# Triangular inverses by 64x64 tiles, eight units a step, with a separate last doubling

## What is computed

```python
# gated delta rule, per head and chunk
a = jnp.where(strict, jnp.einsum("bhncd,bhnsd->bhncs", k_beta, k) * decay, 0.0)
t_inv = lax.linalg.triangular_solve(eye + a, jnp.broadcast_to(eye, a.shape), left_side=True, lower=True)
u = jnp.einsum("bhncs,bhnse->bhnce", t_inv, v_beta)
w = jnp.einsum("bhncs,bhnsd->bhncd", t_inv, k_beta * jnp.exp(g)[..., None])
...
# RWKV-7, per head and token; in chunks it needs such an inverse too
sa = jnp.einsum('bhvk,bhk->bhv', state, a_t)
state = state * w_t[:, :, None, :] + sa[..., None] * b_t[:, :, None, :] + v_t[..., None] * k_t[:, :, None, :]
```

## Time and profile before

| | |
|---|---|
| median of 3 runs | 1961.89 us (1960.22 to 1963.19) |
| the profiled execution | 1957.99 us |
| its span (first to last instruction) | 1956.3 us |
| PE busy | 1835.5 us, 94% |
| PE weight load busy | 1558.4 us, 80% |
| DVE busy | 1059.6 us, 54% |
| ACT busy | 893.8 us, 46% |
| POOL busy | 170.7 us, 9% |
| four batches of the delta rule | about 812 to 1008 us of the span |
| two batches of RWKV | about 1536 to 1650 us |

### The profile page before, as it was taken

One profiled execution on the slowest core, in us unless ns is written; L12 is line 12 of the kernel. 1 busy time (PEld: TensorE's weight loads), 2 busy tenths in 40 slices (PEclk: granted clock), 3 DMA queues, 4 the chain that ended last, 5 costly groups with the idle time before them and its releaser, 6 DMA issues.

```text
span 1956.3 us, 24927 instructions
## 1 busy us (share of the span) xinstructions
PE 1835.5 (94%) x9775; PEld 1558.4 (80%) x9775; DVE 1059.6 (54%) x1591; ACT 893.8 (46%) x1381; POOL 170.7 (9%) x174
## 2 busy tenths in 40 slices
PE   6999999999999999799999999998886787999999
PEld 5888888888888888699988888887765686878887
DVE  4555666555655567633347655566143433456664
ACT  5444555444544476422245544455133111546663
POOL 1000010000000011211012000010101100111220
PEclk9999999999999989899999999999587799999999
DMA  7656656655666554100025665675000000546553
GB/s 231 186 188 188 195 180 193 184 183 182 205 183 188 169 155 144 59 1 1 1 65 178 198 183 185 192 199 181 1 1 1 1 1 1 172 146 190 181 176 105
DMA packets 212870, 262.80 MB, mean 134 GB/s; under 512 B 25947, under 2 KB 149266, under 8 KB 212754
## 3 DMA queue, kind: packets, MB, share of 16 engines
q1 hardware_dynamic: 212754, 261.21, 43.3%
HBM read 260.09 MB, written 1.05 MB: 133 GB/s over the span
## 4 chain that ended last, share of the span: by engine, by line
PE 86%; DVE 8%; ACT 2%; POOL 1%; issue 1%; SPq 1%; DMA 0%; DVEq 0%; ACTq 0%
PE acc L422 21%; PE acc L424 21%; PE acc L423 21%; PE acc L952 3%; PE acc L945 3%; DVE low L396 2%; PE aux L2031 1%; DVE gdn_cv L1228 1%; PE acc L481 1%; PE tr L666 1%; PE aux L930 1%; PE tr L930 1%; PE tr L481 1%; PE tr L494 1%; PE tr L2085 1%
## 5 line engine op out<-in xcount | busy, mean ns | idle before, releaser
L396 DVE TENSOR_TENSOR low<-raw,high 128x1024 fp32r<-128x1024 f32 x487 | 592.5, 1237 | 410.4 <-ACT high L386 403.9
L386 ACT ACTIVATE high<-raw 128x1024 fp32r<-128x1024 f32 x487 | 502.2, 1049 | 411.3 <-PE acc L424 386.9
L422 PE MATMUL acc<-high,xh 128*128 128x512 f32 x1360 | 538.3, 396 | 15.4 <-DVE low L396 11.7
L424 PE MATMUL acc<-high,xl 128*128 128x512 f32 x1360 | 529.4, 389 | 0.0
L423 PE MATMUL acc<-low,xh 128*128 128x512 f32 x1360 | 529.2, 389 | 0.0
L422 PEld LDWEIGHTS acc<-high,xh 128*128 128x128 f32 x1360 | 259.2, 191 | 67.3 <-DVE low L396 12.9
L424 PEld LDWEIGHTS acc<-high,xl 128*128 128x128 f32 x1360 | 259.1, 191 | 53.5
L423 PEld LDWEIGHTS acc<-low,xh 128*128 128x128 f32 x1360 | 259.4, 191 | 49.3
L422 PE MATMUL acc<-high,hh 128*128 128x512 f32 x600 | 237.6, 396 | 3.2 <-DVE hl L1956 3.2
L424 PE MATMUL acc<-high,hl 128*128 128x512 f32 x600 | 234.8, 391 | 0.0
L423 PE MATMUL acc<-low,hh 128*128 128x512 f32 x600 | 234.6, 391 | 0.0
(11 more groups left out here) (418 smaller groups left out, 1884.6 us busy)
## 6 DMA issues: line engine op xcount, KB each, us to landing
raw<-in_ffn_w_gate_up SPq DMA_DIRECT2D x352, 256.0 KB, 3.2
raw<-in_ffn_w_down SPq DMA_DIRECT2D x176, 256.0 KB, 3.1
raw<-in_gdn_w_in SPq DMA_DIRECT2D x96, 256.0 KB, 3.0
raw<-in_ffn_up SPq DMA_DIRECT2D x88, 256.0 KB, 3.1
raw<-in_w_in SPq DMA_DIRECT2D x72, 256.0 KB, 3.3
raw<-in_sc_w_in SPq DMA_DIRECT2D x48, 256.0 KB, 3.1
raw<-in_ffn_down SPq DMA_DIRECT2D x44, 256.0 KB, 3.0
raw<-in_gdn_w_out SPq DMA_DIRECT2D x32, 256.0 KB, 3.0
```

What stands on the lines that cost most here:

```text
L386: nc.scalar.activation(high[t % HIGHS][:, 0:n], raw[t % RAWS][:, 0:n], ACT.Copy).then_inc(high_ready, 1)
L396: nc.vector.tensor_tensor(low[t % RAWS][:, 0:n], raw[t % RAWS][:, 0:n], high[t % HIGHS][:, 0:n].bitcast(F32), ALU.subtract).then_inc(low_r ...
L422: nc.tensor.matmul(o, a, wh, start=(k0 + kk == 0), stop=False)
L424: mm = nc.tensor.matmul(o, b, wh, start=False, stop=(k0 + kk == k - 1))
```

## The change

Everything concerns `Inverse` and what surrounds it.

- U is kept compact, as 64 columns a unit (`Uc` in the delta rule, `U` in the mixer): rows 0 to 63 hold the first diagonal block, rows 64 to 127 the second. `T` and `X` shrink with it. The identity of a compact unit is the new constant `eye`.
- The products of a level work on 64x64 tiles of PE's array: 16 X products (L958 of the changed kernel, 32 moving columns) and 16 U products (L965) for eight units, on the blocks A[rows, rows] of the two diagonal halves. The output of an X product goes to partitions that depend on the unit (`turned`), not on the half that it reads: tiles cross. The transposes turn two compact units at once: 4 a level (L950).
- There is one part of eight units (`parts = (range(8),)`) instead of two halves. DVE has two operations of 128x128 elements after X (L981), and two after U (L991), each pair behind one semaphore from PE; ACT has one copy of T.
- The delta rule's inverse has levels 0 to 5. The last doubling is separate (`last_pe`, `last_act`, `last_dve`, `last_pool`): 4 transposes, 8 products of A's lower left block with the compact U (L1483), a copy by DVE (L1498), 8 products for the corner (L1489), DVE writes it with its sign into the full `U` (L1502), and POOL writes the diagonal blocks of the full U from the compact one, with the masks `lohi` (L1510). DVE's corner waits for POOL's blocks, and PE's V products for both.
- Constants: `eye` and `lohi` are new (three small operations of POOL, one shown); the masks have 6 levels, built at full width and halved by an addition (128x192 elements) at the end.

```diff
-        lvmask = sb("lvmask", [P, 7, 64])
+        eye = sb("eye", [P, 64])
+        lohi = sb("lohi", [P, 2])
+        lvmask = sb("lvmask", [P, 6, 32])
...
-            def __init__(self, tag, n, levels, A, U, T, X):
-                self.n, self.levels, self.A, self.U, self.T, self.X = n, levels, A, U, T, X
-                self.h = n // 2
-                self.bx, self.bu, self.bt = acc[0], acc[1], (aux[0], tr[0])
+            def __init__(self, tag, parts, levels, A, U, T, X, bt, bx):
+                self.parts, self.levels, self.A, self.U, self.T, self.X, self.bt, self.bx = parts, levels, A, U, T, X, bt, bx
...
-            def half(self, h):
-                return range(h * self.h, (h + 1) * self.h)
+            def tiles(self, h):
+
+                for i, j in enumerate(self.parts[h]):
+                    for f in range(2):
+                        yield i, j, f, slice(64 * f, 64 * f + 64), slice(64 * (i % 2), 64 * (i % 2) + 64)
...
-            def turn(self, m, h):
-                for j in self.half(h):
-                    mm = nc.tensor.transpose(self.bt[h][:, (j % self.h) * P:(j % self.h + 1) * P], m[:, j, :], ident[:, :])
+                U = self.U(r)
+                nc.gpsimd.tensor_copy(U[:, :, :], eye[:, :].unsqueeze(1).broadcast_to([P, U.shape[1], 64])).then_inc(self.identity, 1)
+
+            def start_pe(self, pe, r, h):
+                A = self.A(r)
+                for i, j, f, rows, _ in self.tiles(h):
+                    mm = nc.tensor.matmul(self.bt[h][rows, i * 64:(i + 1) * 64], A[rows, j, rows], ident[rows, rows], start=True, stop=True)
+                mm.then_inc(self.x_psum, 1)
...
+            def turn_pe(self, U, h):
+                p = self.parts[h]
+                for i in range(0, len(p), 2):
+                    mm = nc.tensor.transpose(self.bt[h][:, i * 64:(i + 2) * 64], U[:, p[i]:p[i] + 2, :].rearrange("p j c -> p (j c)"), ident[:, :])
                 return mm
...
+            def x_pe(self, pe, r, l, h):
+                A, U = self.A(r), self.U(r)
+                pe.wait_ge(self.u_ready, 2 * self.nth(r, l - 1, h, self.levels))
+                self.turn_pe(U, h).then_inc(self.t_psum, 1)
+                for i, j, f, rows, turned in self.tiles(h):
+                    mm = nc.tensor.matmul(self.bx[h][f][turned, i // 2 * 32:(i // 2 + 1) * 32], A[rows, j, rows], self.second(U[:, :, :], l)[rows, j], start=True, stop=True)
+                mm.then_inc(self.x_psum, 1)
+
+            def u_pe(self, pe, r, l, h):
+                pe.wait_ge(self.x_ready, 2 * self.nth(r, l, h, self.levels))
+                pe.wait_ge(self.t_ready, self.nth(r, l - 1, h, self.levels - 1))
+                for i, j, f, rows, turned in self.tiles(h):
+                    mm = nc.tensor.matmul(self.bx[h][i % 2][rows, 256 + i // 2 * 32:256 + (i // 2 + 1) * 32], self.T[turned, j // 2, f, :],
+                                          self.X[turned, f, j // 2, :], start=True, stop=True)
+                mm.then_inc(self.u_psum, 1)
...
+            def x_dve(self, dve, r, l, h):
+                p = self.parts[h]
+                n = len(p) // 2
+                mask = lvmask[:, l, :].unsqueeze(1).broadcast_to([P, n, 32])
+                dve.wait_ge(self.x_psum, self.nth(r, l, h, self.levels))
+                for f in range(2):
+                    nc.vector.tensor_tensor(self.X[:, f, p[0] // 2:p[0] // 2 + n, :], self.bx[h][f][:, 0:n * 32].rearrange("p (j c) -> p j c", j=n), mask,
+                                            ALU.mult).then_inc(self.x_ready, 1)
...
+            def u_dve(self, dve, r, l, h):
+                p, b = self.parts[h], 1 << l
+                n = len(p) // 2
+                dve.wait_ge(self.u_psum, self.nth(r, l - 1, h, self.levels - 1))
+                for q in range(2):
+                    u = self.second(self.U(r)[:, p[0] + q:p[-1] + 1:2, :], l)
+                    d = self.bx[h][q][:, 256:256 + n * 32].rearrange("p (j k b) -> p j k b", j=n, b=b)
+                    nc.vector.tensor_tensor(u, u, d, ALU.subtract).then_inc(self.u_ready, 1)
...
+                dve.wait_ge(self.x_ready, 2 * self.nth(r, 0, h, self.levels))
+                for q in range(2):
+                    u = self.U(r)[:, p[0] + q:p[-1] + 1:2, 1:64:2]
+                    nc.vector.tensor_tensor(u, u, self.X[:, q, p[0] // 2:p[0] // 2 + n, :], ALU.subtract).then_inc(self.u_ready, 1)
...
-                L, n = self.levels, self.n
-
-                for h in range(2):
-                    self.turn(self.A, h).then_inc(self.x_psum, 1)
+
+                hs = range(len(self.parts))
+                for h in hs:
+                    self.start_pe(pe, r, h)
                 keep_clock(pe, 4)
-                for l in range(1, L):
-                    for h in range(2):
-                        pe.wait_ge(self.u_ready, 2 * (r * L + l - 1) + h + 1)
-                        self.turn(self.U, h).then_inc(self.t_psum, 1)
-                        for j in self.half(h):
-                            c = (j % self.h) * 64
-                            mm = nc.tensor.matmul(self.bx[h][:, c:c + 64], self.A[:, j, :], self.second(self.U[:, :, :], l)[:, j], start=True, stop=True)
-                        mm.then_inc(self.x_psum, 1)
-                    for h in range(2):
-                        pe.wait_ge(self.x_ready, 2 * (r * L + l) + h + 1)
-                        pe.wait_ge(self.t_ready, 2 * (r * (L - 1) + l - 1) + h + 1)
-                        for j in self.half(h):
-                            c = (j % self.h) * 64
-                            mm = nc.tensor.matmul(self.bu[h][:, c:c + 64], self.T[:, j, :], self.X[:, j, :], start=True, stop=True)
-                        mm.then_inc(self.u_psum, 1)
+                for l in range(1, self.levels):
+                    for h in hs:
+                        self.x_pe(pe, r, l, h)
+                    for h in hs:
+                        self.u_pe(pe, r, l, h)
...
+                self.Uc, self.T, self.X, self.X6 = c("gdn_Uc", [8, 64]), c("gdn_T", [4, 2, 64]), c("gdn_X", [2, 4, 32]), c("gdn_X6", [4, 64])
...
-                self.inv = Inverse("gdn_inv", 8, 7, self.A, self.U, self.T, self.X)
-                self.inv.used = self.g_v1_psum
+                self.inv = Inverse("gdn_inv", (range(8),), 6, lambda r: self.A, lambda r: self.Uc, self.T, self.X,
+                                   (aux[0],), acc)
...
+            def last_pe(self, pe, B):
+                pe.wait_ge(self.inv.u_ready, self.inv.all_done(B))
+                lo, hi = slice(0, 64), slice(64, 128)
+                self.inv.turn_pe(self.Uc, 0).then_inc(self.g_last_t, 1)
+                for j in range(8):
+                    turned = slice(64 * (j % 2), 64 * (j % 2) + 64)
+                    mm = nc.tensor.matmul(aux[1][turned, j // 2 * 64:(j // 2 + 1) * 64], self.A[hi, j, lo], self.Uc[hi, j, :], start=True, stop=True)
+                mm.then_inc(self.g_last_x, 1)
+                pe.wait_ge(self.g_last_t_ready, B + 1)
+                pe.wait_ge(self.g_last_x_ready, B + 1)
+                for j in range(8):
+                    turned = slice(64 * (j % 2), 64 * (j % 2) + 64)
+                    mm = nc.tensor.matmul(acc[0][j % 2][lo, j // 2 * 64:(j // 2 + 1) * 64], self.T[turned, j // 2, 0, :], self.X6[turned, j // 2, :], start=True, stop=True)
+                mm.then_inc(self.g_last_u, 1)
+
+            def last_act(self, act, B):
+                act.wait_ge(self.g_last_t, B + 1)
+                nc.scalar.activation(self.T[:, :].rearrange("p j f c -> p (j f c)"), self.inv.bt[0][:, :], ACT.Copy).then_inc(self.g_last_t_ready, 1)
+
+            def last_dve(self, dve, B):
+                dve.wait_ge(self.g_last_x, B + 1)
+                nc.vector.tensor_copy(self.X6[:, :, :].rearrange("p j c -> p (j c)"), aux[1][:, 0:256]).then_inc(self.g_last_x_ready, 1)
+                dve.wait_ge(self.g_last_u, B + 1)
+                dve.wait_ge(self.g_U_diag, 2 * B + 2)
+                for q in range(2):
+                    nc.vector.tensor_scalar(self.U[0:64, q:8:2, 64:128], acc[0][q][0:64, 0:256].rearrange("p (j c) -> p j c", c=64), -1.0, None,
+                                            ALU.mult).then_inc(self.g_U_corner, 1)
+
+            def last_pool(self, pool, B):
+                if B:
+                    pool.wait_ge(self.g_v1_psum, B)
+                pool.wait_ge(self.inv.u_ready, self.inv.all_done(B))
+                for f in range(2):
+                    nc.gpsimd.tensor_scalar(self.U[:, :, 64 * f:64 * f + 64], self.Uc[:, :, :], lohi[:, f:f + 1], None, ALU.mult).then_inc(self.g_U_diag, 1)
...
                 self.inv.pe(pe, B)
-                pe.wait_ge(self.inv.u_ready, 14 * (B + 1))
+                self.last_pe(pe, B)
+                pe.wait_ge(self.g_U_diag, 2 * B + 2)
+                pe.wait_ge(self.g_U_corner, 2 * B + 2)
...
                 self.inv.act(act, B)
+                self.last_act(act, B)
...
                 self.inv.dve(dve, B)
```

(17 more changed lines are left out.)

86 lines of the change are left out of this document (46 added, 40 removed).

## The result

The changed kernel takes 1967.75 us (median of 17 runs, 1966.06 to 1979.11) against 1961.97 us (1959.55 to 1966.00, also 17) for the kernel before on the same chips. The ratio of the means is 1.0035, with a 95% interval from 1.0023 to 1.0047. I had forecast 1921. The change is slower by a third of a per cent where I gave that a chance of one in ten.

What follows compares the result with a forecast made beforehand. PE's 128-column weight loads bound the old levels, the chain through DVE the new. Terms 33.6 + 6.7 - 0.3 - 1.0 - 0.1 = 38.9, plus 1.6 at inverse ends, gave 40.5 us gain: 1921 us, range 1911 to 1951.

Steps and rivals of the forecast that it cites:

- The levels: Levels 1 to 5 of the inverses, 30 in all: 3.22 us each against 4.34, a gain of 33.6 us.
- Rivals 1, 4 and 5: X, U: only two tiles overlap, 1942, 0.12; none overlap, 2001, 0.03; DVE operations take 0.6 us, within 0.2%, 0.03.
- my levels look like the second: Inverse levels, PE busy 65%: clock stays at 1.00, as in an earlier stretch with 2.17 of 3.40 us busy.
- the two cold rivals: Clock at half in part of the inverse levels, 1948, chance 0.13; or through inverses and tail starts, 1985, chance 0.07.
- Rival 3: Clock down through the inverses and each tail's start: levels lose 11 us, starts and tails 12; 1985, chance 0.07.
- PE's waits are 0.55 us at most: Within inverse levels: PE's waits are short, given as a reason against the clock staying down, 1985, chance 0.07.
- The last doubling: End of each delta rule inverse, 4 times: V starts 3.46 us in, gaining 1.67 a batch, 6.7 us in all.
- my bounds: POOL's two diagonal-block operations in the delta rule's last doubling: 0.9 to 2.4 us each, 1.3 taken.
- Batch to batch: Delta rule, one batch's V to the next: 6.6 to 7.4 us less than the 47.95 before.
- unchanged: Delta rule, tail behind each inverse up to the next batch's first products: same length as before.
- The starts: Start of each inverse and of the kernel: losses of 0.3 us in the delta rule, 1.0 mixer, 0.1 kernel start.
- that case's own bounds: Whole kernel, main forecast of 1921 us: 1912 to 1931 with POOL's and DVE's bounds, chance 0.62.

Runs made afterwards that it cites:

- fill_both: The changed kernel plus constant products filling PE's waits in each level and in the last doubling: 1919.45 us, 0.9804 of the kernel before.

## Why the prediction was wrong

- **The levels.** Right in their working. I said 3.22 us; at full clock it is 3.14 to 3.15, with X and U groups of 0.67 (0.74 said) and DVE pairs of 0.49. One can read this in the first level of each batch of the delta rule in the changed kernel and in all its levels in `fill_both`. The small tiles do overlap: 32 passes in 0.67 us, of which the last takes some 0.2, are about 15 ns apart. Rivals 1, 4 and 5 are out.
- **The clock.** This is the step that failed. I set PE's 65% of a level beside one stretch of the earlier trace rows that had kept the clock with 2.17 of 3.40 us, said that "my levels look like the second", and gave the two cold rivals 0.20 together. PE was in fact busy for 1.93 of 3.15 us (61%), and five such levels stand in a row, six times. One stretch that got away with it says little of a row of them; whether the row or the share counts for more, no run here separates. Before the change the inverses had never been run so: PE was busy for 21.67 of 21.70 us there. The fall came in every inverse, in the delta rule behind the first level or the second.
- **The cold rival's price.** Rival 3 had the mechanism, and its 1985 was 17 us too high, by two errors of opposite sign. A cold level is 4.42, not 4.7: PE's groups grew by 0.45, 0.41 and 0.41, 1.27 in all, not 1.5, and 0.08 over the level before, not 0.36. And one or two levels of each inverse were still warm. So the levels, for which it had 11 us lost, gained 12. The tails, for which it had 12 us lost, lost 21 (8.8 in the delta rule, 12.5 in the mixer). Behind the second RWKV inverse alone it was 9.5, where the rival has 2.
- **"PE's waits are 0.55 us at most"** was my reason against that rival, though my own sum has 0.57 between two groups. The waits are 0.61 us and the clock falls all the same. The Trainium skill describes such a loss in "TensorE: Matmul & The Clock Gate", Part 1, as a second way to lose the clock, by frequent micro-idles between groups of products; the trace agrees, with two of 0.61 us in each 3.15. By the same part's rule for practice, to avoid long gaps, the clock would have held; the trace disagrees.
- **The last doubling.** I said V 3.46 us after the last U, a gain of 1.67 a batch. With the clock up it is 4.15, a gain of 0.98. The term that was too small is POOL's pair, 3.10 us against 2.6. It lay inside my bounds (0.9 to 2.4 each, measured 1.55), and the rest of the 0.7 is handoffs. Behind it POOL's masks were hidden, as said.
- **Batch to batch.** I named 6.6 to 7.4 us less from V to V. With the clock up it is 41.18 against 47.95, 6.77 less. In the changed kernel it is 0.25 less, and the 6.5 between them split, in the second batch, into 3.8 for the levels (19.6 us from the first transposes to the last ones, against 15.8), 0.7 for the last doubling (4.81 against 4.15) and the remaining 2.0 for the tail and the next start. That tail is a term that I had put at nothing ("unchanged"), and with the clock down it is 2.2 us a batch.
- **The starts.** The mixer's 32 passes at half clock took 1.97 us (1.9 said). The gain at the kernel's start (0.1) did not come. ACT's first operation behind the masks, at 29.52 before, stands at 31.09 in the changed kernel and at 29.83 to 31.00 in the experiments. That is one execution of each, with a spread that is larger than the term; why it is later is not shown.
- **The time.** With the clock held, the kernel takes 1919.45 where I forecast 1921, with 1912 to 1931 as that case's own bounds. Against the executions of the kernel before taken with it, that is 39.9 us less, where I said 40.5. The sum was right for a clock that the change itself takes away, and in part by luck: the levels gave 2.4 us more than said (1.20 each, not 1.12), the last doublings 2.8 less.
